# Dilated attention's queries and keys accumulated token-major, with their norms' factors applied by token

## What is computed

```python
xn = rms_norm_2(h, norm_mix_g)                       # (256, 1024)
proj = einsum('bsd,de->bse', xn, w_in)
qa, ka, va, c_q, c_kv, k_rope = split(proj)          # widths 512, 512, 512, 768, 256, 32
qa = rms_norm_2(qa.reshape(b, s, 8, 64), qnorm_a_g)  # mean of squares over the 64 of one head and token
ka = rms_norm_2(ka.reshape(b, s, 8, 64), knorm_a_g)
out_a = dilated_attention(qa, ka, va, rel_bias)      # logits q.k / 8 + bias, softmax, times v
# second attention: from c_q and c_kv (the latents), each normed, through w_uq and w_ukv
h = h + einsum('bse,ed->bsd', concat(out_a, out_b), w_o)
# then the feed-forward, and the first block stands in front of all this
```

## Time and profile before

| | us |
|---|---|
| three runs, median | 813.55 |
| the profiled execution | 811.38 |
| its span | 809.6 |
| TensorE busy (matmuls) | 801.1 |
| VectorE busy | 573.8 |
| ScalarE busy | 462.6 |
| GpSimd busy | 102.7 |

### The profile page before, as it was taken

One profiled execution on the slowest core, in us unless ns is written; L12 is line 12 of the kernel. 1 busy time (PEld: TensorE's weight loads), 2 busy tenths in 40 slices (PEclk: granted clock), 3 DMA queues, 4 the chain that ended last, 5 costly groups with the idle time before them and its releaser, 6 DMA issues.

```text
span 809.6 us, 13913 instructions
## 1 busy us (share of the span) xinstructions
PE 801.1 (99%) x5972; PEld 709.1 (88%) x5972; DVE 573.8 (71%) x719; ACT 462.6 (57%) x606; POOL 102.7 (13%) x80
## 2 busy tenths in 40 slices
PE   9999999999999999999999999999999999999998
PEld 7999988788888998888888799997899988888886
DVE  6868995996666677666676687699867865555653
ACT  7679774564534674545545565456787644444442
POOL 1102780671000000000000010000430000000000
PEclk9999999999999999999999999999999999999999
DMA  9744443444553555555455554545322555555541
GB/s 325 290 157 167 163 166 133 157 158 155 170 207 114 234 178 188 179 204 191 177 205 187 181 204 166 208 157 160 134 85 98 215 172 193 208 175 189 208 156 52
DMA packets 36221, 143.05 MB, mean 177 GB/s; under 512 B 9362, under 2 KB 11426, under 8 KB 22208
## 3 DMA queue, kind: packets, MB, share of 16 engines
q1 hardware_dynamic: 34976, 138.69, 49.0%
q0 software_dynamic: 1040, 3.43, 1.2%
q10 hardware_dynamic: 144, 0.04, 0.0%
HBM read 141.08 MB, written 1.06 MB: 176 GB/s over the span
## 4 chain that ended last, share of the span: by engine, by line
PE 94%; ACT 2%; DMA 2%; DVE 1%; issue 1%; SPq 1%; POOL 0%
PE ps L1900 8%; PE ps L1901 7%; PE ps L1902 7%; PE ps L2310 7%; PE ps L2303 7%; PE ps L2215 6%; PE ps L2217 6%; PE ps L2216 6%; PE ps L1968 5%; PE ps L1971 5%; PE ps L1974 5%; PE ps L2308 4%; PE ps L2305 4%; PE ps L2076 2%; DMA raw<-w 1%; PE ps L1926 1%
## 5 line engine op out<-in xcount | busy, mean ns | idle before, releaser
L1117 DVE TENSOR_TENSOR wlo<-raw,whi 128x2048 fp32r<-128x2048 f32 (+1 forms) x128 | 291.1, 2276 | 86.9 <-ACT whi L586 85.6
L586 ACT ACTIVATE whi<-raw 128x2048 fp32r<-128x2048 f32 (+1 forms) x128 | 242.6, 1896 | 117.8 <-DMA raw<-w 117.6
L1900 PE MATMUL ps<-xx,whi 128*128 128x256 f32 x504 | 145.0, 288 | 1.0 <-issue 0.7
L1901 PE MATMUL ps<-xx,whi 128*128 128x256 f32 x504 | 142.6, 283 | 0.0
L1902 PE MATMUL ps<-xx,wlo 128*128 128x256 f32 x504 | 142.5, 283 | 0.0
L1900 PEld LDWEIGHTS ps<-xx,whi 128*128 128x128 f32 x504 | 96.6, 192 | 2.5 <-issue 1.3
L1901 PEld LDWEIGHTS ps<-xx,whi 128*128 128x128 f32 x504 | 96.6, 192 | 0.1
L1902 PEld LDWEIGHTS ps<-xx,wlo 128*128 128x128 f32 x504 | 96.6, 192 | 0.0
L2215 PE MATMUL ps<-whi,xx 128*128 128x512 f32 x216 | 84.1, 390 | 0.0
L2216 PE MATMUL ps<-whi,xx 128*128 128x512 f32 x216 | 84.1, 389 | 0.0
L2217 PE MATMUL ps<-wlo,xx 128*128 128x512 f32 x216 | 84.0, 389 | 0.0
(11 more groups left out here) (314 smaller groups left out, 1310.4 us busy)
## 6 DMA issues: line engine op xcount, KB each, us to landing
raw<-w SPq DMA_DIRECT2D x109, 1024.0 KB, 4.8
raw<-w SPq DMA_DIRECT2D x34, 512.0 KB, 4.9
raw<-w SPq DMA_DIRECT2D x8, 256.0 KB, 5.5
x<-xT SPq DMA_DIRECT2D x4, 256.0 KB, 5.5
work<-bias_scratch POOLq DMA_DIRECT2D x1, 1024.0 KB, 7.9
raw<-w SPq DMA_DIRECT2D x4, 192.0 KB, 3.3
out<-x SPq DMA_DIRECT2D x3, 256.0 KB, 2.5
raw<-w SPq DMA_DIRECT2D x3, 240.0 KB, 3.5
```

What stands on the lines that cost most here:

```text
L586: A(hi, full, ACT.Copy).then_inc(sem("hi_ready"), 1)
L1117: V.tensor_tensor(lo, full, hi.bitcast(F32), ALU.subtract)\
L1900: mm(out, hi, xh[:, tile, :], start=start, stop=False, skip_group_check=skip)
L1901: mm(out, hi, xl[:, tile, :], start=False, stop=False, skip_group_check=skip)
```

## The change

Queries and keys are accumulated by `token_major`, in pairs, from weights loaded in half rows. ScalarE reads each pair's two banks four times when the pair is complete: a square and a copy for each half of the tokens, both scaled by the token's factor. VectorE sums the squares of each head along the free axis and adds epsilon; GpSimd raises the sums to -0.5, queries and keys each in one instruction (16 numbers a partition), in the same buffer as before. The keys are multiplied by their factor token-major on VectorE. Then 8 transposes turn the queries, between the keys' two units, and 8 turn the keys, at the place of `dilated_bc`. VectorE copies the turned queries out of banks 5 and 6, ScalarE the turned keys out of banks 3 and 4, with the gains. The two groups of small sums, the Newton steps and the spread are gone. `latent_stats` comes after the first 12 matmuls of the queries and `latent_bc` after their first unit. Some semaphores are shared (sgb_in with sgw_in, bias_in with scr_out), so that their waits count to 32; the lines are left out here.

```diff
 def by_rows(u):
-    return U_GA <= u < U_WB or U_WA <= u < U_WOUT
+    return U_GA <= u < U_WB or U_WA <= u < U_WOUT or U_QA <= u < U_KR or U_KA <= u < U_VA
+def row_pair(u):
+    first = U_KA if U_KA <= u < U_VA else u - u % 2
...
         qa, ka = view(8, 4), view(12, 4)
-        sqA, kxA = view(16, 8), view(16, 4, 512)
+        qa_sq, ka_sq = view(16, 4, 512), view(20, 4, 512)
+        ka_tok, qa_tok = view(72, 4, 512), view(76, 4, 512)
         va, vb = view(24, 4, 512), view(28, 4, 512)
...
         ms, rh = (nt[:, 2 * i:2 * i + 2, :].rearrange("p a n -> p (a n)") for i in range(2))
+        ms2, rh2 = (v[:, 0:32].rearrange("p (s h) -> p s h", s=2) for v in (ms, rh))
         LATENTS = (3, 0, 1, 2)
...
                 if by_rows(u):
+                    first, half = row_pair(u)
                     for i in range(2):
                         dst = raw[:, u % SLOTS, 1024 * i:1024 * i + 1024].rearrange("p (n c) -> p n c", n=2)
-                        src = w[stored(u - u % 2 + i)].rearrange("p (n c) -> p n c", n=2)[:, :, columns(u % 2)]
+                        src = w[stored(first + i)].rearrange("p (n c) -> p n c", n=2)[:, :, columns(half)]
                         sp.dma_start(dst, src).then_inc(sem(f"raw_in{u % SLOTS}"), 16)
                 elif U_UQ <= u < U_WO:
...
                 pool.wait_ge(sem(name + "_fac"), turn)
+            def dilated_factors(part):
+                pool.wait_ge(sem("sa_eps"), part + 1)
+                hs = slice(8 * part, 8 * part + 8)
+                nc.gpsimd.tensor_tensor(rh2[:, :, hs], ms2[:, :, hs], half_s[:, 0:1].unsqueeze(1).broadcast_to([P, 2, 8]), ALU.pow)\
+                    .then_inc(sem("sa_fac"), 1)
             def rotate(g, t):
...
+            dilated_factors(0)
+            dilated_factors(1)
             head_factors("sk", 32, 16)
...
-            def heads_sq(m):
-                evacuated((U_QA, U_QA + 1, U_KA, U_KA + 1)[m])
-                A(sqA[:, 2 * m:2 * m + 2, :], (qa if m < 2 else ka)[:, 2 * (m % 2):2 * (m % 2) + 2, :], ACT.Square)\
-                    .then_inc(sem("qk_sq"), 1)
+            def heads_evac(u0, dst, sq):
+                filled(u0 + 1)
+                for t in range(2):
+                    A(sq[:, t, :], ps[(u0 + t) % RING][:, :], ACT.Square, scale=rtok[:, 2, t:t + 1]).then_inc(sem("sa_sq"), 1)
+                for t in range(2):
+                    evac(u0 + t, dst[:, t, :], ACT.Copy, scale=rtok[:, 2, t:t + 1])
+            def heads_keys(j):
+                act.wait_ge(sem("sa_turned"), 3 + j)
+                A(ka[:, 2 * j:2 * j + 2, :], two(ps[3 + j][:, :]), ACT.Copy, scale=gqk[:, 0:1]).then_inc(sem("ka_n"), 1)
             def latents_hi(i):
...
             ahead(U_QA)
-            heads_sq(0)
-            heads_sq(1)
             latents_hi(1)
             latents_hi(2)
+            heads_evac(U_QA, qa_tok, qa_sq)
             act.wait_ge(sem("vb_mm"), 1)
             evac(U_KR, vb[:, 0, :], ACT.Copy, b=(U_KR + 1) % RING)
...
             A(cosk[64:96, 0, :], ang[64:96, 0, :], ACT.Sin).then_inc(sem("sin"), 1)
-            heads_sq(2)
             ahead(U_KA)
-            heads_sq(3)
             ahead(U_KA + 1)
+            heads_evac(U_KA, ka_tok, ka_sq)
             ahead(U_VA)
             act.wait_ge(sem("half"), 1)
             A(warm[:, :], half_s[:, 0:1], ACT.Exp)
+            heads_keys(0)
+            heads_keys(1)
             def softmax_exp(p):
...
-            def scaled_heads(m):
-                scaled((U_QA, U_QA + 1, U_KA, U_KA + 1)[m], (qa if m < 2 else ka)[:, 2 * (m % 2):2 * (m % 2) + 2, :])
+            def dilated_sums(part):
+                dve.wait_ge(sem("sa_sq"), 2 * part + 2)
+                sums = ms2[:, :, 8 * part:8 * part + 8]
+                link(V.reduce_sum(sums, (qa_sq, ka_sq)[part].rearrange("p s (h c) -> p s h c", c=64), AX))
+                V.tensor_scalar(sums, sums, *((1.0, 64 * EPS), (1.0 / 64, EPS))[part], ALU.mult, ALU.add).then_inc(sem("sa_eps"), 1)
+            def heads_queries():
+                for j in range(2):
+                    dve.wait_ge(sem("sa_turned"), 1 + j)
+                    V.tensor_copy(qa[:, 2 * j:2 * j + 2, :], two(ps[5 + j][:, :])).then_inc(sem("qa_n"), 1)
+            def heads_scaled():
+                dve.wait_ge(sem("sa_fac"), 2)
+                for t in range(2):
+                    evacuated(U_KA + t)
+                k4 = ka_tok.rearrange("p s (h c) -> p s h c", c=64)
+                V.tensor_tensor(k4, k4, rh2[:, :, 8:16].unsqueeze(3).broadcast_to([P, 2, HEADS, 64]), ALU.mult).then_inc(sem("ka_s"), 1)
             def latents(i):
...
-            scaled_heads(0)
             dve.wait_ge(sem("norm_bcs"), before("bcs", "c") + 1)
             latents(0)
             latents_lo(0)
             ahead(U_QA)
-            scaled_heads(1)
             latents(1)
             latents(2)
...
             latents_lo(1)
             latents_lo(2)
+            dilated_sums(0)
             ahead(U_QA + 1)
...
             ahead(U_KR)
-            scaled_heads(2)
-            scaled_heads(3)
+            heads_queries()
             rotary()
             ahead(U_KA)
-            dve.wait_ge(sem("sa_stats"), 1)
-            st2 = ps[7][:, 0:32].rearrange("p (s h) -> p s h", s=2)
-            ms2 = ms[:, 0:32].rearrange("p (s h) -> p s h", s=2)
-            link(V.tensor_scalar(ms2[:, :, 0:8], st2[:, :, 0:8], 64.0, 64.0 * EPS, ALU.mult, ALU.add))
-            link(V.tensor_scalar(ms2[:, :, 8:16], st2[:, :, 8:16], EPS, None, ALU.add))
-            v, y, f, a = (nt[:, i, :] for i in range(4))
-            link(V.tensor_scalar(nti[:, :], v.bitcast(I32), 1, None, ALU.logical_shift_right))
-            link(V.tensor_scalar(y.bitcast(I32), nti[:, :], -1.0, 1597463007.0, ALU.mult, ALU.add))
-            for it in range(3):
-                link(V.tensor_tensor(a, y, y, ALU.mult))
-                link(V.scalar_tensor_tensor(rs[:, :], a, -0.5, v, ALU.mult, ALU.mult))
-                link(V.scalar_tensor_tensor(f if it == 2 else y, rs[:, :], 1.5, y, ALU.add, ALU.mult))
-            V.tensor_copy(kxA.rearrange("p s (h w) -> p s h w", h=HEADS),
-                          rh[:, 0:32].rearrange("p (s h) -> p s h", s=2)[:, :, 8:16].unsqueeze(3).broadcast_to([P, 2, HEADS, 64]))\
-                .then_inc(sem("sa_kx"), 1)
+            dilated_sums(1)
             ahead(U_KA + 1)
-            for b in range(2):
-                dve.wait_ge(sem("sa_bc"), b + 1)
-                V.scalar_tensor_tensor(ka[:, 2 * b:2 * b + 2, :], ka[:, 2 * b:2 * b + 2, :], gqk[:, 0:1],
-                                       two(ps[3 + b][:, :]), ALU.mult, ALU.mult).then_inc(sem("ka_n"), 1)
+            heads_scaled()
             ahead(U_VA)
-            dve.wait_ge(sem("bias_in"), 16)
+            dve.wait_ge(sem("scr_out"), 32)
             def keys_sums():
...
-                if i not in (3, 14):
-                    return
-                half = i // 12
-                pe.wait_ge(sem("qk_sq"), 2 + 2 * half)
-                if half == 0:
-                    pe.wait_ge(sem("norm_bcs"), before("bcs", "c") + 1)
-                for s in range(2):
-                    for j in range(4 * half, 4 * half + 4):
-                        c = 2 * j
-                        last = token_sums(ps[7], 16 * s, sqA[:, j, :], s * P, cst_s[:, C_Z64 + 16 - c:C_Z64 + 32 - c], width=16,
-                                          start=j == 0 and s == 0, stop=j == 7, skip_group_check=True)
-                if half:
-                    last.then_inc(sem("sa_stats"), 1)
-            def dilated_bc():
-                pe.wait_ge(sem("sa_kx"), 1)
-                for j in range(4):
-                    for s in range(2):
-                        last = nc.tensor.transpose(ps[3 + j // 2][:, (j % 2) * T + s * P:(j % 2) * T + (s + 1) * P],
-                                                   kxA[:, s, j * P:(j + 1) * P], ident)
-                    if j % 2:
-                        last.then_inc(sem("sa_bc"), 1)
+            def dilated_turned(tok, bank):
+                for c in range(4):
+                    for t in range(2):
+                        last = nc.tensor.transpose(ps[bank + c // 2][:, (c % 2) * T + t * P:(c % 2) * T + (t + 1) * P],
+                                                   tok[:, t, c * P:(c + 1) * P], ident)
+                    if c % 2:
+                        last.then_inc(sem("sa_turned"), 1)
+            def queries_ready():
+                for u in (U_QA, U_QA + 1):
+                    pe.wait_ge(sem(f"evac{u % RING}"), FILLS[u][u % RING] + 1)
+                dilated_turned(qa_tok, 5)
+            def keys_ready():
+                pe.wait_ge(sem("ka_s"), 1)
+                dilated_turned(ka_tok, 3)
             first_unit(U_CQ, 8, "n5")
             two_tiles(U_CQ + 1, 8, between=lambda: norm_stats("n5", sq3))
             two_tiles(U_CQ + 2, 8, between=lambda: norm_bc("n5"))
             two_tiles(U_CKV, 8)
-            two_tiles(U_QA, 8, between=latent_stats)
```

(9 more changed lines are left out.)

14 lines of the change are left out of this document (7 added, 7 removed).

## The result

The changed kernel takes 820.52 us (median of 6 executions, 817.92 to 821.46) against 812.55 us for the kernel before beside it (6 executions, 811.12 to 815.53). The ratio is 1.009 with an interval of 1.0074 to 1.0106: slower by 0.9%, where the prediction said 815.5 us and a range up to 819.0. The profiled execution took 820.26 us, its span 818.4 us.

What follows compares the result with a forecast made beforehand. TensorE, busy 99% of the span, was taken as the bound. Against 2.43 us less work stood waits of 2.3, 0.5 and 3.5 us and 0.2 of restarts; the 4.15 us shift gave 815.5 us, range 811.5 to 819.0.

Steps and rivals of the forecast that it cites:

- TensorE's work: Query, key and value units: matmuls 1.28 us less, small sums 2.03 less, transposes 0.88 more; 2.43 us less in all.
- First wait: Ahead of the first vb product, TensorE idles 2.3 us until ScalarE's first copy frees the queries' bank.
- Second and third wait: Keys: about 0.5 us mid-values for VectorE's split of unit 90, then 3.5 us at the key transposes for the factor chain.
- The power: GpSimd's power for the keys' factor takes 3.55 us, from the row of 16 elements a partition.
- I add nothing: Keys' power beside VectorE's split of unit 91: up to 1.2 us longer by the skill's rule, counted as 0.
- The clock: Behind TensorE's waits: the forecast sum has no term for a slower clock; it read 1.00 in every stretch.
- rival (e): After 3.5 us idle TensorE runs at half pace for as long again: 2.2 us on top, 817.7 us; chance 0.15.
- the prediction's own signs of being wrong: No wait gap, a power under 2 us, clock below 1.00 behind the gap, or a like loss elsewhere.
- (b): GpSimd's power takes 1.65 us, everything behind it comes 1.9 us earlier: shift 2.25, 813.6 us; chance 0.15.
- (c): Attention gives back part of the shift, at most 1.38 us of TensorE idle: 814.1 to 815.5 us; chance 0.15.
- (d): Key factors ready before TensorE asks, chain shorter by all 6.3 us of waits: 809.0 us; chance 0.10.

Runs made afterwards that it cites:

- the last reordering: Changed kernel, ScalarE's query squares and copies first, VectorE's keys' sum and unit-90 split before rotary, ScalarE's key squares and copies before rounding unit 91: 811.39 us, ratio 0.9987.
- the fitting fillers: Changed kernel with 9 identity products on TensorE ahead of the first vb product and 12 ahead of the key transposes: 817.07 us, ratio 1.0063.
- the second profile of the changed kernel: The changed kernel measured and profiled once more, unaltered: 820.69 us, ratio 1.0095 against the kernel before.
- the two reordered kernels: Changed kernel with ScalarE's query copies first and VectorE's keys' sum ahead of rotary, without and with ScalarE's key copies before rounding unit 91: 812.04 and 811.39 us.
- the kernel with late keys: Changed kernel with key transposes behind all values' matmuls and unit 91's products ahead of the first queries-keys product: 817.06 us, one execution.

## Why the prediction missed, by its own steps

**TensorE's work: right.** The four units run at 0.227 us per matmul of 512 columns. Once most waits are out of the way (the last reordering), the stage is 0.98 us shorter than before with 0.88 us of wait left in it, so 1.9 us of the 2.43 us are there. Another 0.16 lie ahead of the cut, because the sums come behind 12 x 0.2267 us of the queries and no longer behind 24 x 0.120. The rest, some 0.4, I put down to restarts after a wait and between groups, which I had only partly counted; no run shows it.

**First wait: right in place, cause and size** (2.13 us for 2.3), and the cause was shown by moving ScalarE's copies.

**Second and third wait: right in mechanism.** Where neither a slow clock nor the first wait precedes them, they measure 0.49 and 3.46 us for 0.5 and 3.5. In the changed kernel the third is 2.78 and the second doesn't show, because TensorE itself comes later: behind the first wait it ran at half pace. Of the 8 slow matmuls' 8 x (0.427 - 0.2267) = 1.6 us most comes back there, as the wait would have held TensorE anyway: of the 6.5 us, 4.7 are the waits (the fitting fillers) and 1.6 the last slow stretch, which leaves 0.2 us for the first one. These 0.2 are what it delays the copy of vb (1.85 - 1.66 us). The same delay was 0.3 us larger in the second profile of the changed kernel, so the first stretch's price is not fixed. One slip: from its own terms TensorE reaches the second wait at 552.56 and not 552.66; it changes nothing that follows.

**The power: two errors that nearly cancel.** The undisturbed price is 2.90 us, not the 3.55 of the row with 16 elements, and beside a split it is 3.80. The row was no undisturbed one: it began beside a split, and so did the two rows of 8 elements, each beside one of 2.28 us (timelines of VectorE and GpSimd, kernel before):

```profile
570.59 0.95 DVE L1117 TENSOR_TENSOR wlo<-raw,whi 128x768 fp32r<-128x768 f32 x1
```
```profile
570.76 3.55 POOL L547 TENSOR_TENSOR nt<-nt,half_s 128x16 f32<-128x16 f32 x1 [49.84 <-DVE nt L1752]
```

So the equal 3.55 us of 8 and of 16 elements were two different sums, and the 1.65 us of the other 8-element row were the price where no split was running at the start. "I add nothing" was the wrong choice between row and rule. The Trainium skill (GPSIMD Engine Reference, Specifications) has the two engines contend when VectorE reads two SBUF inputs, and the trace agrees: 0.9 us more beside a split of 1.22 us (3.80 against 2.90). The sum was 0.25 us too low at this step.

**The clock: the step that failed.** The forecast put the clock's fall behind the waits at nothing; it stood only in rival (e), with a chance of 0.15 and a price of 2.2 us. The runs show 1.8 us in its place, the largest single term that the sum lacks, and a clock below 1.00 behind the gap was one of the prediction's own signs of being wrong. TensorE had no idle time of this size before, so no row could tell, and I let "no row shows it" weigh as if it meant "unlikely". It happened in both profiles of the changed kernel, behind both waits. Its price at the last wait is 1.6 us (5.36 us from the transposes to the first product against 3.77 in the edits without a slow stretch there), 1.8 in all by the kernel with fitting fillers. The Trainium skill (TensorE: Matmul & The Clock Gate, Why this matters for your kernels) warns of idle gaps between bursts; here the clock fell after gaps of 2.1 and 2.8 us. The rival had the fall right, but not its length: it wrote "for as long again" as the idle time, and the slow matmuls lasted 3.4 us behind 2.13 us of idling and 3.3 us behind 2.78. Nor do its 2.2 us follow from that: they are the loss of the 22 small matmuls of the start (4.41 us at half pace), while 3.5 us at half pace would lose 1.75.

**The sum and its base.** By steps: 4.15 forecast, +0.6 for what the waits cost beyond it (45.2 - 40.48 = 4.7), +1.8 for the clock makes 6.5, as measured. The measured time is 5.0 us above the forecast: 1.2 are the base (812.55 for 811.38), 0.6 the waits, 1.8 the clock. The remaining 1.5 us, between 6.5 and the medians' 8.0 (7.5 in the second comparison), lie ahead of the stage by the two profiles; the late weights are the largest item seen there, and their cause stays open. The range's upper end, 819.0, would have just missed even a time made of steps and clock alone (812.55 + 6.5 = 819.05), since I had set it as if rival (e) and a high base excluded each other.

**The chances.** Slower had 0.40 and within half a per cent 0.55. The forecast stood exactly on the bound, and nearly every cost left out (restarts, clock, sharing) pointed up. The skew should have gone to slower.

**Rivals.** (b) a power of 1.65 us: no. (c) part given back in attention: no, from the first product of queries and keys on both kernels take the same time within 0.33 us. (d) keys ready in time: not in this order, but the two reordered kernels come close to it, with 0.9 us of wait.

## What to carry to other kernels

On an engine that is 99% busy, price a new wait of 2 us or more with its length and, as a term of the sum, with a slow stretch behind it (in this stage one followed eight of nine such waits), and treat two such waits as linked: removing one may only show the other. Before taking a duration from a row, look what the neighbouring engine was doing when that instruction started. When work moves from a busy engine's own chain to one over three engines (here bank, ScalarE, VectorE, GpSimd, VectorE), write down for each link what stands ahead of it in its queue; the same instructions in another order were worth 9.3 us here (820.69 against 811.39 in one comparison; 7.9 of it in the stage), from 0.9% slower to about even. Work that saves 2.4 us on the bounding engine is not a gain until its inputs come 2.4 us earlier.

## What the runs showed of the hardware

- TensorE's granted clock fell from 2.4 to 1.2 GHz (0.427 us per matmul of 512 columns for 0.227) after eight idle times of 2.13 to 3.12 us in this stage, and the slow matmuls lasted about 3.4 us each time; after waits of 1.79 us and less in the same stage no profile shows a fall. Elsewhere one does: the kernel with fitting fillers had a fall from 470.3 to 473.7 us behind an idle time of 1.47 us, while 1.58 us near 312 us in the changed kernel had none. It did not fall after 3.46 us in one execution (most others of that kernel had a lower mean clock), nor after the 3.05 us in the softmax of the kernel with late keys, where the stretch from 570 to 580 us reads 1.00. What decides it stays open.
- A power over 128x16 elements on GpSimd took 2.90 us alone, 2.92 with a split only in its last 0.6 us, 3.53 to 3.55 when it began beside a VectorE split of 0.95 us, 3.80 beside one of 1.22 us, and 4.87 to 4.89 beside one of 2.29 us, with or without a second one behind it. In all these cases it ended 2.75 to 2.78 us behind the split that was running at its start. One over 128x8 took 1.63 us alone (at 201.00 us in the kernel before), and 3.55 when it began beside a split of 2.28 us; the earlier trace rows has the means.
- A float32 product of the 128x128 identity shows as two matmuls of 0.11 us; a filler counted as one is twice too long.
- Where a matmul waits for several things, the releaser that the trace infers can be an engine that merely finished at about that time: it named VectorE where the wait was for ScalarE's copy.
